# A projection whose activations come turned from the host, with the norm's factors put to the products, in a fused encoder kernel

## The reference, cut to what matters

```python
def rms_norm(x, g):
    y = x * rsqrt(mean(x * x, axis=-1) + 1e-6)
    return y * g

h = rms_norm(x, g_mix)                  # x: (2048, 1024)
z = h @ w_in                            # w_in: (1024, 1536)
c_val, c_gate, s_in = z[:, :512], z[:, 512:1024], z[:, 1024:]
u = c_val * sigmoid(c_gate)             # goes to the causal convolution
# s_in goes to the diagonal state-space mixer
```

## Time and profile before

| what | value |
|---|---|
| median of 3 executions | 2018.83 us (2012.39 to 2023.08) |
| profiled execution, its own time | 2024.83 us |
| its span in the profile | 2023.3 us |
| busy in the span: PE, PEld, DVE, ACT, POOL | 84%, 77%, 56%, 40%, 28% |
| first product of the projection, first product of round 1, last product | 24.71, 65.98, 325.83 us |

### The profile page before, as it was taken

How to read it: one execution, slowest core, us unless ns; L and a number is a source line. 1 busy time by engine, 2 the same in 40 slices (tenths; PEclk the granted TensorE clock), 3 DMA queues, 4 the chain that set the end, 5 groups by cost and what they waited for, 6 DMA issues and landing times. The chain is left out here.

```text
span 2023.3 us, 33770 instructions
## 1 busy us (share of the span) xinstructions
PE 1705.8 (84%) x11301; PEld 1547.9 (77%) x11302; DVE 1126.5 (56%) x1855; ACT 813.4 (40%) x1063; POOL 574.4 (28%) x883
## 2 busy tenths in 40 slices
PE   6999996977475599999963999999999999999980
PEld 6999996955364478777753999988998888988970
DVE  6323212543364477777743664664566788666655
ACT  4222210223111234333221664664555777555553
POOL 0476773000243211454523121121211211121220
PEclk9999997578687699898876999999999999999995
DMA  7422115443995333332234887886688999888858
GB/s 217 130 95 94 71 65 119 91 132 118 264 311 145 92 115 112 108 95 94 92 152 165 268 287 236 282 283 229 209 278 301 307 376 374 264 271 276 280 164 342
DMA packets 179951, 399.74 MB, mean 198 GB/s; under 512 B 82063, under 2 KB 118929, under 8 KB 152752
## 3 DMA queue, kind: packets, MB, share of 16 engines
q1 hardware_dynamic: 154112, 332.17, 47.1%
q0 software_dynamic: 20080, 58.34, 11.9%
q10 hardware_dynamic: 5696, 8.39, 1.6%
HBM read 309.72 MB, written 89.13 MB: 197 GB/s over the span
## 5 line engine op out<-in xcount | busy, mean ns | idle before, releaser
L1681 DVE TENSOR_TENSOR expert_lo<-expert_raw,expert_hi 128x2048 fp32r<-128x2048 f32 x192 | 430.6, 2285 | 47.2 <-ACT expert_hi L1677 47.0
L1677 ACT CAST expert_hi<-expert_raw 128x2048 fp32r<-128x2048 f32 x192 | 361.8, 1911 | 17.6 <-DMA expert_raw<-in_experts 9.5
L554 PE MATMUL proj_p_z<-proj_h_hi,proj_w_hi 128*128 128x256 f32 x768 | 219.7, 286 | 9.6 <-DVE proj_u_out L495 7.7
L555 PE MATMUL proj_p_z<-proj_h_lo,proj_w_hi 128*128 128x256 f32 x768 | 217.8, 284 | 0.0
L556 PE MATMUL proj_p_z<-proj_h_hi,proj_w_lo 128*128 128x256 f32 x768 | 217.7, 283 | 0.0
L2081 PE MATMUL moe_p_g0u<-expert_hi,moe_xh 128*128 128x256 f32 x736 | 210.2, 286 | 1.5 <-DVE moe_xl L1994 1.5
L2082 PE MATMUL moe_p_g0u<-expert_hi,moe_xl 128*128 128x256 f32 x736 | 205.9, 280 | 0.0
L2083 PE MATMUL moe_p_g0u<-expert_lo,moe_xh 128*128 128x256 f32 x736 | 205.8, 280 | 0.0
L2096 PE MATMUL moe_p_y<-expert_hi,moe_hh 128*128 128x512 f32 x368 | 153.2, 416 | 13.0 <-DVE moe_hl L2005 13.0
L554 PEld LDWEIGHTS proj_p_z<-proj_h_hi,proj_w_hi 128*128 128x128 f32 x768 | 147.8, 193 | 11.2 <-issue 11.2
L1923 POOL DMA_INDIRECT residual<-moe_y,moe_ids_s x46 | 78.5, 1708 | 259.5 <-ACT moe_y L1950 252.5
(11 more groups left out here) (432 smaller groups left out, 4239.6 us busy)
## 6 DMA issues: line engine op xcount, KB each, us to landing
expert_raw<-in_experts SPq DMA_DIRECT2D x192, 1024.0 KB, 7.8
ffn_input<-mix_h SPq DMA_DIRECT2D x17, 512.0 KB, 4.0
proj_x_sb<-in_x SPq DMA_DIRECT2D x8, 1024.0 KB, 5.6
mix_x_sb<-in_x SPq DMA_DIRECT2D x16, 512.0 KB, 5.5
residual<-mix_x SPq DMA_DIRECT2D x16, 512.0 KB, 2.7
out<-final_x SPq DMA_DIRECT2D x16, 512.0 KB, 5.9
proj_w_raw<-in_w_in SPq DMA_DIRECT2D x8, 768.0 KB, 7.5
final_x<-residual SPq DMA_DIRECT2D x3, 2048.0 KB, 16.4
```

Source lines behind the costliest of these rows:

```text
L554: nc.tensor.matmul(o, whi, h_hi[:, half, c], start=c == 0 if start is None else start, stop=False)
L555: nc.tensor.matmul(o, whi, h_lo[:, half, c], start=False, stop=False)
L1677: self.nc.scalar.copy(self.hi[:, u], self.raw[:, u]).then_inc(self.hi_done, 1)
L1681: tensor_tensor(self.lo[:, u], self.raw[:, u], self.hi[:, u].bitcast(FP32), ALU.subtract).then_inc(self.lo_done, 1)
```

## The change

- The host hands x over a second time, turned: for each round 128 channels in the partitions, then chunk and token (`x_turned`). Gain, taps (reversed, channel in the partition) and decay rates come in their final layout as well.
- `high` and `low` split the turned x as it is, 2048 columns at once, from one buffer (`x_raw`); round 0 in two halves (`low_first`). The transposes of x, `scale_x`, and the small products for taps and decay rates are gone.
- The channel gain goes into the weights: `high_w` is a scaled activation, `low_w` a scalar_tensor_tensor in place of a tensor_tensor.
- The token factors go to the products. `factors` scales the identity by them (`scales`), one fp32 matmul with a matrix of ones (`spread_factors`) spreads them over all partitions, ScalarE copies them to SBUF (`spread_factor`), and VectorE multiplies each PSUM bank by them as it reads it (`scaled`): two banks straight into `s_out`, four into a double buffer `z`. Gate and gated product then read and write SBUF.
- Each unit of a round waits for its own bank (`z_read`) in place of the wait for all of them at the head.
- The block of constants becomes part of GpSimd's stream in `projection`. Three small loads go to ScalarE's queue. In SP's stream the first weights stand before x.
- `chunk_turn` moves ahead of `low(1, 1)`, so before round 1 and before the gated products of round 0; `magnitude` stands behind chunk 2, `factors(0)` behind chunk 4.

```diff
@@ constants, projection @@
+def constants(nc, pool, cleared, built, ident, eye_turn, lagged, ones):
+    nc.gpsimd.memset(ident[:, :], 0.0).then_inc(cleared, 1)
+    nc.gpsimd.memset(lagged[:, :, :], 0.0).then_inc(cleared, 1)
+    nc.gpsimd.memset(ones[:, :], 1.0).then_inc(cleared, 1)
+    nc.gpsimd.memset(eye_turn[:, :], 0.0).then_inc(cleared, 1)
+    pool.wait_ge(cleared, 4)
+    step = Chain(pool, built)
...
+            def load_w(c):
                 if c >= RAW:
                     sp.wait_ge(w_lo_done, c - RAW + 1)
                 sp.dma_start(w_raw[:, c % RAW], w_rows[c]).then_inc(w_read[c % RAW], 16)
-            sp.dma_start(x_sb[:, 1], x_rows[1]).then_inc(x_in[1], 16)
-            sp.wait_ge(taps_laid, 1)
+            def load_turned(n):
+                sp.wait_ge(lo_done, n + 1)
+                sp.dma_start(x_raw[:, :, :], x_turned[n]).then_inc(turned_in, 16)
+            def load_x(n):
+                wait(sp, squared, n * 2)
+                sp.dma_start(x_sb[:, :, :], x_rows[n]).then_inc(x_in, 16)
+            sp.dma_start(gain[:, :], g_mix).then_inc(gain_in, 16)
+            load_w(0)
+            sp.dma_start(x_raw[:, 0:HALF], x_turned[0][:, 0:HALF]).then_inc(first_in, 16)
+            load_w(1)
+            sp.dma_start(x_raw[:, HALF:KD], x_turned[0][:, HALF:KD]).then_inc(turned_in, 16)
+            load_w(2)
+            load_x(0)
+            for c in range(3, KD):
+                load_w(c)
+            load_turned(1)
+            load_x(1)
...
+                if more:
+                    load_turned(n + 2)
+                    load_x(n + 2)
...
+            def high(n, half):
+                act.wait_ge(turned_in, n * 16 + 16)
+                wait(act, z_done, (n - 1) * UNITS)
+                nc.scalar.copy(x_hi[:, half], x_raw[:, :, :]).then_inc(hi_done, 1)
+            def spread_factor(n, half):
+                act.wait_ge(spread, n + 1)
+                nc.scalar.copy(factor[:, half], p_f[:, 0:NK]).then_inc(factor_done, 1)
+            def gate(n, j):
+                act.wait_ge(z_read, n * UNITS + (3 + j))
+                gate_part = z[:, j % 2, NK:2 * NK]
+                nc.scalar.activation(gate_part, gate_part, ACT.Sigmoid).then_inc(sig_done, 1)
+            def high_w(c):
+                act.wait_ge(w_read[c % RAW], 16 * (c // RAW + 1))
+                nc.scalar.activation(w_hi[:, c], w_raw[:, c % RAW], ACT.Copy, scale=gain[:, c:c + 1]).then_inc(w_hi_done, 1)
...
+            lam_rows = ((lam[:, :, :], lam_in), (dt[:, :], log_dt.partition_broadcast(P)))
+            for to, rows in lam_rows:
+                act.dma_start(to, rows).then_inc(lam_read, 16)
+            act.wait_ge(cleared, CONSTANTS)
+            act.dma_start(lagged[:, :, TB - 1:TB - 1 + TAPS], conv_w).then_inc(taps_in, 16)
             act.wait_ge(gain_in, 16)
+            high_w(0)
+            act.wait_ge(first_in, 16)
+            nc.scalar.copy(x_hi[:, 0, 0:HALF], x_raw[:, 0:HALF]).then_inc(hi_done, 1)
+            high_w(1)
+            act.wait_ge(turned_in, 16)
+            nc.scalar.copy(x_hi[:, 0, HALF:KD], x_raw[:, HALF:KD]).then_inc(hi_done, 1)
+            for c in (2, 3):
+                high_w(c)
             square(0, 0)
...
+            for c in range(4, KD):
+                high_w(c)
+            spread_factor(0, 0)
+            high(1, 1)
+            square(1, 1)
             def body(n, half, more):
                 if more:
+                    high(n + 1, 1 - half)
                     square(n + 1, 1 - half)
...
+                for j in range(CT):
+                    gate(n, j)
+                    if j == 1 and more is not None:
...
+            def factors(n):
                 step = Chain(dve, own, n * (RSQRT_STEPS + 1))
                 dve.wait_ge(squared, n * 2 + 2)
...
+                step(V.tensor_scalar(stat[:, 1], stat[:, 0], 1.0 / D, EPS, ALU.mult, ALU.add))
+                rsqrt(nc, step, stat[:, 3], stat[:, 1], stat[:, 2], stat[:, 0])
                 for h in range(2):
...
+                    last = V.tensor_scalar(scales[:, h], ident[:, :], stat[:, 3, h:h + 1], None, ALU.mult)
+                last.then_inc(scales_done, 1)
+            def low(n, half):
+                dve.wait_ge(hi_done, n + 2)
+                V.tensor_tensor(x_lo[:, half], x_raw[:, :, :], x_hi[:, half].bitcast(FP32),
+                                ALU.subtract).then_inc(lo_done, 1)
+            def low_first(i):
+                dve.wait_ge(hi_done, i + 1)
+                part = slice(i * HALF, (i + 1) * HALF)
+                V.tensor_tensor(x_lo[:, 0, part], x_raw[:, part], x_hi[:, 0, part].bitcast(FP32),
+                                ALU.subtract).then_inc(lo_done, 1)
+            def low_w(c):
+                dve.wait_ge(w_hi_done, c + 1)
+                V.scalar_tensor_tensor(out=w_lo[:, c], in0=w_raw[:, c % RAW], scalar=gain[:, c:c + 1],
+                                       in1=w_hi[:, c].bitcast(FP32), op0=ALU.mult, op1=ALU.subtract).then_inc(w_lo_done, 1)
+            def scaled(n, half, j):
+                dve.wait_ge(z_done, n * UNITS + (j + 1))
+                if j == 0:
+                    dve.wait_ge(factor_done, n + 1)
+                    wait(dve, s_stored, n * 16)
+                if j >= 2:
+                    wait(dve, u_done, n * CT + (j - 3))
+                to = s_out[:, 2 * j:2 * j + 2] if j < 2 else z[:, j % 2].rearrange("p (c k) -> p c k", c=2)
+                V.tensor_tensor(to, p_z[j][:, :].rearrange("p (c k) -> p c k", c=2),
+                                factor[:, half].unsqueeze(1).broadcast_to([P, 2, NK]), ALU.mult).then_inc(z_read, 1)
+            def glu(n, j):
+                dve.wait_ge(sig_done, n * CT + (j + 1))
+                if j == 0:
+                    wait(dve, u_stored, n * 16)
+                V.tensor_tensor(u_out[:, j], z[:, j % 2, 0:NK], z[:, j % 2, NK:2 * NK], ALU.mult).then_inc(u_done, 1)
             dve.wait_ge(gain_in, 16)
...
+            low_w(0)
+            low_first(0)
+            low_w(1)
+            low_first(1)
+            dve.wait_ge(lam_read, 32)
+            for c in range(2, KD):
+                low_w(c)
+                if c == 2:
                     magnitude(turn_step)
+                if c == 4:
+                    dve.wait_ge(built, 1)
+                    factors(0)
                 if c == 5:
                     angle(turn_step)
+            chunk_turn(turn_step)
+            low(1, 1)
+            factors(1)
             def body(n, half, more):
                 if more:
...
+                    low(n + 1, 1 - half)
+                    dve.wait_ge(spread, n + 1)
+                    factors(n + 1)
+                for j in (0, 1, 2, 3):
+                    scaled(n, half, j)
+                for j in (4, 5):
+                    glu(n, j - 4)
+                    scaled(n, half, j)
+                for j in (2, 3):
+                    glu(n, j)
...
+            def spread_factors(n):
+                pe.wait_ge(scales_done, n + 1)
+                wait(pe, factor_done, n)
+                nc.tensor.matmul(p_f[:, 0:NK], ones[:, :], scales[:, :, :].rearrange("p h k -> p (h k)"),
+                                 start=True, stop=True).then_inc(spread, 1)
             def first_products():
-
-                pe.wait_ge(lo_done, 4)
                 for c in range(KD):
                     pe.wait_ge(w_lo_done, c + 1)
+                    if c % HALF == 0:
+                        pe.wait_ge(lo_done, c // HALF + 1)
                     for j, blocks in enumerate(units):
                         for b, m in enumerate(blocks):
-
                             last = product(p_z[j][:, b * NK:(b + 1) * NK], m, c, 0,
                                            start=c == 0 and b == 0, stop=c == KD - 1 and b == 1)
                         if c == KD - 1:
                             last.then_inc(z_done, 1)
-                    if KD - 3 <= c < KD - 1:
-                        transposes(1, 1, range(2 * (c - KD + 3), 2 * (c - KD + 3) + 2))
+                    if c == KD - 2:
+                        spread_factors(0)
             def products(n, half, more):
-                pe.wait_ge(lo_done, n * 4 + 4)
+                pe.wait_ge(lo_done, n + 2)
                 for j, blocks in enumerate(units):
...
+                    pe.wait_ge(z_read, n * UNITS + (j + 1 - UNITS))
                     for b, m in enumerate(blocks):
-                        o = p_z[j][:, b * NK:(b + 1) * NK]
                         for c in range(KD):
-                            last = product(o, m, c, half)
+                            last = product(p_z[j][:, b * NK:(b + 1) * NK], m, c, half, start=c == 0, stop=c == KD - 1)
                     last.then_inc(z_done, 1)
...
+                    if more and j == 3:
+                        spread_factors(n + 1)
             first_products()
+            spread_factors(1)
...
+    x_chunks = _np.asarray(inputs["x"])[0].reshape(NK, T8, KD, P)
```

(62 more changed lines are left out.)

179 lines of the change are left out of this document (43 added, 136 removed).

## The result

The changed kernel took 2003.43 us, the median of 10 runs (1998.42 to 2007.7), against 2020.49 (2012.16 to 2025.74, 10 runs) for the kernel before beside it: ratio 0.9921, 95% interval 0.9902 to 0.9941. It is faster by 17.1 us, more than the 10 us of the bound; the forecast was 1995, the range 1987 to 2008 holds the time. The time lies above the forecast case's 1990 to 1999. The profiled execution took 2003.85 us, its span 2002.4, so 20.9 less than the span before.

A forecast was written before the change was run, and what follows sets the result against it. TensorE's projection products bound the kernel, GpSimd's turn tables 14 us behind. After the change both ways end near 306 (306.1, 305.8), taken as 307.4, 24 us earlier: 2018.8 - 24 = 1995 us, range 1987 to 2008.

The forecast's parts named there:

- the first case: Projection: TensorE's and GpSimd's ways both end the stage near 306; gain 20 to 29, 1990 to 1999 us; chance 0.53.
- the rival of a slower start: Kernel start: chunk 0 lands 4.4 us later behind small transfers; gain 15 to 19, 2000 to 2004 us; chance 0.14.
- One sign named for a wrong prediction: Behind the projection: the prediction is wrong if the stages behind 307 change length.
- TensorE's way: Projection products: round 1 starts at 52.6, last product ends at 299.9, next stage's first transfer at 306.1.
- the order the prediction named: Before round 1, ScalarE: high of round 1 stands behind the copy of round 0's factors, high to 46.4, low to 48.7.
- The loss to the clock after the pause: TensorE after its pause before round 1: lower clock rate costs 1.5 us, bounds 0 and 3.5.
- The start: Queue and round 0: chunk 0 lands at 5.3, first product about 11, VectorE's chain 36.5 us, turn8 ready about 45.
- GpSimd's way: Turn tables: start at 45, 242 us of units plus 18 of meetings, end at 305, next stage 305.8.
- the parts of the 18: GpSimd's loss to VectorE instructions with two SBUF operands: 12.4 us from seven subtractions, 6.0 from 32 gated products.
- The end of the stage: Projection's end: GpSimd's last store lands some 3.5 us after its issue ends, next stage's transfer 0.8 us later.
- the rival of GpSimd alone: Turn tables alone end the stage, losing 29.5 us to VectorE; gain 14, 2005, or gain 10, 2009; chance 0.20.
- The finer wait: Start of each projection round: TensorE's wait for the last gated product goes, 1.2 us a round, 7.2 in six rounds.

The follow-up runs named there:

- ScalarE's order: Changed kernel with ScalarE's high(1, 1) and square(1, 1) put ahead of the copy of round 0's factors; 2001.54 us.
- the second turn buffer and no low parts read: Changed kernel with a second turn-table buffer for GpSimd and zeros written for the low parts of x in rounds 1 to 7; 2005.71 us.
- both ways shortened: Changed kernel plus second turn buffer, late small loads, ScalarE's order, and VectorE's low(1, 1) and factors(1) ahead of chunk_turn; 2001.02 us, repeated 1991.97 us.
- small loads later: Changed kernel with the loads of decay and step moved from ScalarE's queue to SP's, behind the third weight chunk; 2004.09 us.
- chunk's turn late: Changed kernel with chunk_turn put back behind factors(1) and the gated products of round 0; 2018.47 us.
- no low parts read: Changed kernel with VectorE writing zeros instead of subtracting for the low parts of x in rounds 1 to 7; 2002.4 us.
- second turn buffer: Changed kernel with GpSimd's table units alternating between two buffers, each waiting for the stores of the last but one; 2008.28 us.
- the finer wait alone: Kernel before, transposes kept, with TensorE waiting bank by bank instead of for all output copies, and a ScalarE sigmoid-buffer wait; 2006.84 us, ratio 0.9945.

## Why the prediction was right, and where its terms were off

The mechanism was right: the two ways end the stage close to each other, and its steps are in the trace. The time is another matter. A gain of 17.1 us is below the first case (20 to 29), and 2003.4 falls into the numbers of the rival of a slower start (2000 to 2004), which is true only in part: the start was 2.7 us late and not 4.4. The range holds the time because it was drawn over the rivals. One sign named for a wrong prediction came true: the stages behind the projection changed length. In the profiled executions the convolution took 2.7 us less, and what lies between it and the last norm 2.0 more.

**TensorE's way.** Right nearly throughout. From the last product of round 0 at 51.0 it pauses for 3.3 us (forecast 3.8); `high(1, 1)` ran at 47.29 behind the copy of the factors at 47.02 and made VectorE wait 1.54 us, the order the prediction named, and the run with ScalarE's order showed it. No middle round waits. The spreading matmul costs 0.42 instead of 0.6. The loss to the clock after the pause was put at 1.5 us: from round 1's start to its spreading matmul, 55.32 to 79.92, are 24.60 us against 23.04 of products (192 steps of 0.120), 1.56 more. The windows show it as granted clock:

```profile
54.00:56.00 2.00, 1.37 (x8) 1.01 (x9) 1.97 (x6) 0.00 (x0) 1.34 (x7) 1.00 1.03 225
56.00:58.00 2.00, 2.00 (x13) 2.00 (x12) 0.96 (x2) 1.54 (x2) 1.53 (x7) 0.54 0.92 299
58.00:60.00 2.00, 2.00 (x13) 2.00 (x13) 1.60 (x4) 1.14 (x4) 1.67 (x5) 0.61 0.95 383
60.00:62.00 2.00, 2.00 (x19) 2.00 (x18) 1.51 (x3) 1.35 (x2) 1.63 (x5) 1.00 0.96 300
```

TensorE had stood since 51.3; the work began again at 54.63, the grant fell shortly behind 56, was at the lower level of 1.2 GHz (0.50) from 56.4 to 59.5, and was back at 60. This term was not the same in every run. The same stretch took 25.37 us, 2.33 more than its products, in the run with the second turn buffer and no low parts read, where the grant had fallen before the work began, and 23.10 us, nothing lost, with ScalarE's order, after a pause of 1.93 us. Both runs with both ways shortened, with pauses of 2.18 and 2.27 us, lost nothing either (23.11). Last product 301.2 against 299.9, next stage by this way 307.2 against 306.1.

**The start.** This term failed: chunk 0 landed at 8.03 instead of 5.3, so that everything behind moved by 2.8 us. VectorE's chain itself was right: from 11.01, without idle time, to 47.68 (47.49 and 0.19), 36.7 us against 36.5. The rate of a full queue was used for a stretch with 223 GB/s. Of the 2.7 us the run with later small loads showed 1.9 to be the small transfers' doing; the rival of a slower start had named them. The other 0.8 stays open; the third small load, of the taps, stayed on ScalarE's queue in that run.

**GpSimd's way.** It started at 47.9 instead of 45. Up to the end of the last issue it took 255.8 us; forecast were 256.5 (242 + 18 less the landing of 3.5). A unit took 32.7 us on average (48.6 to 277.3, seven units), as forecast. But the parts of the 18 were not right. Seven subtractions cost 14.7 us together, not 12.4. One meeting as the trace shows it:

```profile
49.22 2.30 DVE L484 TENSOR_TENSOR proj_x_lo<-proj_x_raw,proj_x_hi 128x2048 fp32r<-128x2048 f32 x1 [1.54 <-ACT proj_x_hi L355]
...
49.19 0.20 POOL L126 TENSOR_TENSOR proj_tt<-proj_turn 128x4 f32<-128x4 f32 x1
49.47 2.12 POOL L127 TENSOR_TENSOR proj_turn<-proj_tt 128x4 f32<-128x4 f32 x1
```

An operation of 4 elements that takes 0.20 us otherwise took 2.12, to the end of VectorE's. That leaves little for the 32 gated products (6.0 forecast). The way of all eight units grew by 13.1 us against before (70.31 to 312.98, 242.7), less than the subtractions' share alone. With no store waited for and no low parts read it took 215.4 us (47.82 to 263.18), and before, less 25.9 us of waits for its stores, 216.8. So the gated products, which had one operand in PSUM before, cost GpSimd nothing that these two numbers show. VectorE's own gated product between 70 and 300 us went from 0.42 to 0.57 us on average. The rule of the Trainium skill, SBUF — State Buffer, section "Who interferes with whom", that the second waits for the whole of the first, fits the large instructions (14.7 of 16.1 us); its result for all 39 of them, 29.5 us and a stage end near 317, did not come.

**The end of the stage.** The step that cost most. It was taken that the last store lands 3.5 us behind the end of its issue and that 0.8 us follow. The trace gives each transfer's time from the start of its issue to its landing. In the changed kernel it is 5.3 and 4.0 us for the last two stores:

```profile
turn_sin<-proj_turn POOLq DMA_DIRECT2D x1, 512.0 KB, 5.3
conv_input<-proj_u_out SPq DMA_DIRECT2D x1, 512.0 KB, 4.0
```

The same for all ends of the stage (us; "landed" is the start of the issue plus that time):

| kernel | GpSimd's last store issued, landed | SP's last store issued, landed | next stage | behind the later landing |
|---|---|---|---|---|
| changed | 303.10, 308.4 | 303.14, 307.1 | 311.15 | 2.8 |
| small loads later | 302.74, 307.6 | 302.06, 305.1 | 310.40 | 2.8 |
| ScalarE's order | 303.96, 307.8 | 301.55, 304.5 | 310.51 | 2.7 |
| chunk's turn late | 318.52, 322.3 | 304.40, 307.3 | 325.05 | 2.7 |
| no low parts read | 301.68, 305.7 | 303.02, 307.0 | 308.45 | 1.4 |
| second turn buffer | 277.30, 281.1 | 302.84, 305.7 | 307.19 | 1.5 |
| before | 312.43, 318.0 | 327.01, 329.9 | 331.36 | 1.5 |

Two things were mis-sized. First, the landing: a last store of SP by itself takes 2.9 us and GpSimd's second one 3.8, but 5.3 where GpSimd's two and SP's went out together, 1.5 MB (between 304 and 308 the DMA share was 0.98). Even in the kernel before, GpSimd's last store landed at 318.0 and not at 316.5. Second, what follows: 1.4 to 1.5 us where SP's store lands last and 2.7 to 2.8 where GpSimd's does. Why the latter is longer the traces don't show. In the run with no low parts read SP's store landed last, so there it was TensorE's way that ended the stage. The forecast of 305.8 for GpSimd's way became 311.15: 2.9 from the start, -0.7 from the way, 3.2 from the end (1.2 from the landing, 2.0 behind it).

I took 307.4 for the stage end because two ways near each other rarely both come early, and it was 3.8 short. The first case (both ways together, gain 20 to 29) held in the trace at its lower edge, 20.2, and not in the medians; the rival of GpSimd alone was right on who is last and wrong on why: not the meetings, but the late start, the landing and what follows it.

**From the stage to the total.** The forecast, 1994.8 before rounding, and the measured 2003.4 differ by 8.6 us: 3.8 from the stage end; -0.7 from the stages behind it, where the trace shows 20.9 in sum against 20.2; 3.8 because the profiled executions differ by 20.9 and the medians by 17.1; 1.7 because the ten runs of before have a median of 2020.5 and not 2018.8.

**The finer wait** was put at 1.2 us a round. A round start with it is 1.25 us cheaper: from the first product behind a group of transposes to the next such one across it 25.15 us (90.75 to 115.90) became 23.90 (88.87 to 112.77). Seven times that is 8.8 us, and the stage gained 9.5. Of the other 0.7 the first product's earlier place is 0.2 (24.50 against 24.71), and the wait before round 1, 1.40 us in the earlier trace rows and not 1.02, is 0.4.

## What to carry to other kernels

Before pricing a large rewrite, try its smallest part alone: here one wait per bank in place of one for all gave almost half of the gain of the stage. When two engines are both near the end of a stage, shortening one gains only up to the other: here 4.0 us for GpSimd's way alone, 0.6 for TensorE's alone, and 7.9 to 8.0 for both ways and the start together. Price the end itself in two parts, from the last store's issue to its landing and from there to the first transfer behind it, for each engine that may issue it and with the stores that go out beside it. When a unit of work becomes faster, look at what its stores now meet. In the first microseconds of a kernel a small transfer on another queue isn't free if a large one is waited for.

## What the runs showed of the hardware

The same matmuls of the stage behind the change ran at different granted clocks in different kernels. The first 93 us of the convolution and the next 92 (window, length, PE, PEld, DVE, ACT, POOL busy, granted clock, DMA share, GB/s), before the change:

```profile
331.36:424.36 93.00, 72.97 (x341) 68.94 (x342) 50.20 (x67) 19.09 (x15) 7.79 (x3) 0.52 0.59 128
424.36:516.36 92.00, 66.19 (x373) 43.70 (x372) 33.32 (x44) 29.15 (x37) 0.00 (x0) 0.83 0.40 123
```

After the change:

```profile
311.15:404.15 93.00, 60.64 (x340) 56.16 (x340) 49.90 (x67) 18.80 (x15) 7.79 (x3) 0.61 0.58 127
404.15:496.15 92.00, 63.47 (x375) 43.01 (x373) 33.52 (x44) 29.24 (x38) 0.00 (x0) 0.85 0.43 127
```

With the second turn buffer:

```profile
307.19:400.19 93.00, 73.21 (x341) 69.03 (x342) 50.18 (x67) 19.08 (x15) 7.79 (x3) 0.52 0.58 127
400.19:492.19 92.00, 66.14 (x373) 43.61 (x371) 33.31 (x44) 29.09 (x37) 0.00 (x0) 0.83 0.39 123
```

With the kernel before released bank by bank:

```profile
321.83:414.83 93.00, 61.30 (x348) 57.50 (x349) 50.76 (x68) 18.96 (x15) 7.79 (x3) 0.62 0.59 128
414.83:506.83 92.00, 61.08 (x366) 41.58 (x365) 32.65 (x43) 29.13 (x37) 0.00 (x0) 0.86 0.46 130
```

The same 340 or so matmuls keep TensorE busy for 73 us in two of them and for 61 in the other two. Before the change the grant stayed at 0.50 (1.2 GHz) from 351 to 391, in windows in which TensorE was busy all the time; after it, it rose to 1.00 some 40 us into the stage, under the same matmuls. The state-space stage's first load comes 180.7, 178.0, 180.8 and 175.6 us after the convolution's first transfer in these four, and the differences of PE busy in the second stretch (66.2, 63.5, 66.1, 61.1) are as large. So 2.7 us of the changed kernel's profiled gain came from here, the second turn buffer lost 2.8 in the same place, and the finer wait alone gained 5.1. The repeated runs of the changed kernel (178.0 and 177.9) and of the one with both ways shortened (178.1 twice) agree. Over all twelve traces the stage takes between 175.2 and 180.8 us, and not in the order of its start: 175.2 from 310.51 (ScalarE's order), 175.5 from 310.40 (small loads later), 178.0 from 311.15. What decides it was not tried and stays open. From there to the last norm's first load the same code took between 1462.0 us (finer wait) and 1472.0 (both ways shortened, first time; 1467.5 the second), 1464.2 before and 1466.1 after the change, and why stays open. With the second turn buffer it took 1471.8: its total is thus -4.0 in the stage, +2.8 and +5.7 behind it, which is why its span of 2006.8 is above 2002.4. The finer wait alone, 10.7 us later at the stage's end than the change, got 2.5 and 4.1 of that back behind it, so the share of almost half holds for the stage and is a larger one in the total (11.3 us against 15.0 on the same chip, with intervals that overlap).
